# Two transformer layers and a mixture-of-experts block on one core: attention taken chunk by chunk, the second chunk moved beside the first chunk's gathers

## The chip, the cores and the metric

The kernel runs on one core of one Trainium2 chip. The metric is the device time of one execution in microseconds; lower is better. The core has TensorE (PE, matrix products; its weight loads are PEld), VectorE (DVE), ScalarE (ACT), GpSimd (POOL) and SyncE (SP), and 16 DMA engines that all queues share. SP issues the loads and stores of whole blocks, POOL the gathers of rows by index. All numbers are float32.

## The reference

256 tokens of width 1024 (two chunks of 128) go through two layers and then through one block of another kind. Shortened, one layer is:

```python
proj = h @ w_in[l]                        # 1024 -> 1536: qa ka va qb kb vb
qa = rope(rms_norm(qa, qn_g)); ka = rope(rms_norm(ka, kn_g))   # 8 and 2 heads of 64
oa = softmax(qa ka^T / 8) va              # branch 0: all 256 keys
ob = window_sink_attention(qb, kb, vb)    # branch 1: distance bias, |i-j| <= 128, sink
oa = rms_norm(oa, gn_a_g); ob = rms_norm(ob, gn_b_g)           # per head of 64
h = layer_norm(ALPHA * h + concat(oa, ob) @ w_o[l], ln1)
q = h @ peer_wq[l]                        # 1024 -> 2048 = 8 heads x 2 halves x 128
s = q . sub_keys                          # 8 x 2 x 128 scores per token
top 16 of each half, top 16 of the 256 sums -> 128 experts per token
a = gelu(u[expert] . h);  ffn = sum_k softmax(s)_k a_k v[expert_k]
h = layer_norm(ALPHA * h + ffn, ln2)
```

Queries need only their own chunk of tokens; keys and values of both chunks are needed by every query. After the two layers come modulation columns (silu of a condition vector times a 1024 x 6144 matrix), a context of 256 rows that is turned into states of two recurrent mixers, the mixers over the tokens, and 64 experts of which each token uses 8.

## The kernel before

Every engine has a program of its own (`tensor_program`, `vector_program`, `scalar_program`, `gpsimd_program`, `sync_program`). Each runs its instructions in the order in which the Python code emits them. What must wait for another engine names an event (`at("ps", "proj", l, i, c)`), and the wait stands in the order of the waiting engine: all that is queued behind it waits too. L123 is a line of the kernel; most operations are recorded at the line of a helper (L155 matmul, L158 transpose, L76 to L118 DVE, L125 ACT, L134 POOL, L2424 the gather, L1343 the dot product).

For each layer `attention(l)` runs first, for both chunks: h is turned (`hT`), three blocks of `w_in` give the projections of both chunks, `rope` normalizes and rotates queries and keys (DVE one half, POOL the other), `turned_heads` turns each head of 64 by itself, then `scores`, `exps`, `turned_powers` and `values` for two branches and two chunks. The softmax's divisor is applied to the values; `squared` and `normed` make the RMS norm in rows (token by token), the result is turned again (`mT`) and multiplied with `w_o`, and a layer norm follows for each chunk. In layer 0 the twelve blocks of the modulation matrix (`mod_products`, 2 MB each, two places in the ring) are woven between these steps by hand.

Then `peer(l, background)` runs: queries of both chunks (`queries(i, c)`, four blocks of `peer_wq`, each used for both chunks) and key scores in halves, in the order (half 0, chunk 0), (half 0, chunk 1), (half 1, chunk 0), (half 1, chunk 1). DVE's `route(0)` finds the experts of the first 64 gathers as soon as half 0 of chunk 0 is there. Then 256 gathers run, 128 for each chunk: gather n fetches 128 rows of 8 KB (u and v of one expert for each token). DVE takes the dot product of its first half with h (`dots`), ACT makes gelu, weight and a diagonal matrix (`weigh`), PE adds the weighted second half to two accumulators in PSUM (`weighted_sum`). There are eight landing places (`GATHERS`), and POOL issues gather n when PE has used gather n - 8. Between gathers each engine takes pieces of `route(q + 1)` (DVE, every second gather) and of a background generator: `beside(l, n)` says after which gathers one piece is taken. In layer 0 the background is the context's rows and features (40 places, every sixth gather), in layer 1 the context's states (80 places, every third gather, from 10 on). A piece is the same step of one list on every engine.

The ring is 20 places of 4 KB per partition in SBUF for weights and landings, the arena 88 KB per partition for everything else. `sync_program` is one list of loads in a fixed order; each waits for the place that it overwrites, and all loads behind it wait with it.

```python
                for n in range(256):
                    if n % 128 == 0:
                        two = [fresh("acc", l, n // 128, x, among=SUMS[n // 128]) for x in range(2)]
                    weighted_sum(n, two)
                    advance(background, beside(l, n))
```

Of the kernel before, what the change touches and what calls it, by code (L numbers as in the profile page):

```python
# [5 lines left out]
P = 128  # L6
# [188 lines left out]
WQ_AT = (4, 8, 16, 0)  # L195
UNITS = [(0, 0), (0, 1), (1, 0), (1, 1)]
ROUTE_PIECES, EXP_AT, WEIGHTS_AT = 24, 50, 54
NORM_AT = (130, 131, 133, 137, 138)


def beside(l, n):

    if l:
        return 1 if n in range(10, 250, 3) else 0
    return 1 if n in range(10, 246, 6) else 0
# [16 lines left out]
class Side:  # L222


    def __init__(self, x, ar, o, t, rows, convs, convs2=(), convs3=()):
# [3 lines left out]
        self.x, self.tag, self.ar, self.t = x, "x" if x else "ctx", ar, t  # L229
# [8 lines left out]

    def T(self, i, n=1):
        return self.ar(self.t + 512 * i, 512 * n)  # L240
# [58 lines left out]
def build(nc, d, out):  # L299
    import numpy as np  # L300
    ctx = ExitStack()
    with ctx:
# [9 lines left out]
        s_x0, s_cst = [sem(f"x{c}_loaded") for c in range(2)], sem("constants_loaded")  # L312
# [5 lines left out]
        s_gab, s_ctx = sem("gab_loaded"), sem("context_loaded")  # L318
        s_featured, s_feat = sem("features_stored"), sem("features_loaded")
# [40 lines left out]
        def R(i, k):  # L360
# [3 lines left out]
                                                  "b_mod", "cvec", "conv", "norm_cols")}  # L364
        asm = {n: sm(k) for n, k in (("ss0", 10), ("rs0", 10), ("ss1", 10), ("rs1", 10), ("s8", 8))}
        for i in range(2):
            asm |= {f"{n}{i}": sm(k) for n, k in (("ms", 16), ("mr", 16))}
# [14 lines left out]
        ctx_side = Side(False, ar, {"Rk": 9600, "Rv": 10624, "GG": 11648, "GkT": 13696}, 16768,  # L382
                        [("Rk", 0, 16), ("Rv", 1, 16)], [(0, "Gk", 16, 4), (1, "Gv", 16, 8)])
        ctx_rows = ar(11648, 2048).rearrange("p (c n) -> p c n", c=2)
        hcT = ar(14720, 2048).rearrange("p (k t) -> p k t", k=8)
        ctx_tiles = [ar(14720 + 512 * i, 512) for i in range(11)] + [ar(512, 512), None]
        ctx_kd = ar(0, 512)
        ctx_features = ar(9600, 5120)
        norm_scratch = ar(2048, 1024)
        SC = ar(0, 4096)  # L390
        gs, aa = ar(9056, 256), ar(9312, 256)
        diagonals = [ar(8800, 64), ar(8928, 64)]
        mod_rows = ar(20480, 2048)
        silu_cols = ar(19840, 256).rearrange("p (k s) -> p k s", k=8)

        def landing(n):

            i = n % GATHERS
            return R(4 + 2 * i, 2) if i < 5 else ar(6144, 2048) if i == 5 else R(2 * i - 12, 2)
# [2505 lines left out]
```

## Time and profile before

| | us |
|---|---|
| median of 3 runs (2923.17 to 2926.06) | 2924.0 |
| profiled execution, its own time | 2928.04 |
| span of the profiled execution, first to last instruction | 2926.2 |

| engine | busy us | share of the span |
|---|---|---|
| PE | 2148.5 | 73% |
| PEld | 1089.7 | 37% |
| DVE | 1582.8 | 54% |
| ACT | 813.4 | 28% |
| POOL | 843.2 | 29% |

The page also cuts the span into 40 slices of 73 us; each digit is the busy share in tenths (9 is 90% or more), for PEclk the granted clock of TensorE in tenths of full speed, and the last line is what the DMA engines moved.

```profile
PE   6988677666766989676767666789878677667573
DVE  4426857678544645888979865455552522121111
PEclk9889687677866989688888997899989788888887
DMA  7744999999999414999999999412112599999994
GB/s 282 263 169 159 421 422 422 420 412 395 422 422 378 194 37 160 381 421 375 413 378 403 422 421 417 159 42 74 58 62 101 210 404 401 388 391 381 382 379 146
```

The shares are averages over stages with different limits, so they say little by themselves. The stages are told apart by the gathers: slices 4 to 12 and 15 to 24.

### The profile page before, as it was taken

How to read it: one execution, taken by the hardware profiler on the slowest of the kernel's cores; microseconds unless marked ns; L12 is line 12 of the kernel's file. 1: busy time of each engine (PE TensorE's matmuls, PEld its weight loads, DVE VectorE, ACT ScalarE, POOL GpSimd, SP SyncE). 2: the span in 40 equal slices, each digit the busy share in tenths (PEclk: the TensorE clock that was granted, in tenths of full speed). 3: DMA queues.
4: the chain of work that ended last, by engine and by line, in shares of the span. 5: the costliest groups of instructions: out<-in, count | busy, mean ns of one | idle time of the engine just before them, and what ended most of it. 6: DMA issues, size and time to landing. Idle time of an engine off the chain costs nothing.

```text
span 2926.2 us, 33545 instructions
## 1 busy us (share of the span) xinstructions
PE 2148.5 (73%) x11740; PEld 1089.7 (37%) x11740; DVE 1582.8 (54%) x3254; ACT 813.4 (28%) x2292; POOL 843.2 (29%) x723
## 2 busy tenths in 40 slices
PE   6988677666766989676767666789878677667573
PEld 3657111121211559232323221568764532222221
DVE  4426857678544645888979865455552522121111
ACT  1402343433433212343343533322210111111110
POOL 1001444445432100454445553012110111222221
PEclk9889687677866989688888997899989788888887
DMA  7744999999999414999999999412112599999994
GB/s 282 263 169 159 421 422 422 420 412 395 422 422 378 194 37 160 381 421 375 413 378 403 422 421 417 159 42 74 58 62 101 210 404 401 388 391 381 382 379 146
DMA packets 130146, 891.48 MB, mean 305 GB/s; under 512 B 23216, under 2 KB 23600, under 8 KB 31792
## 3 DMA queue, kind: packets, MB, share of 16 engines
q0 software_dynamic: 86976, 553.74, 46.9%
q1 hardware_dynamic: 42992, 335.50, 28.6%
q8 instruction: 95, 1.56, 0.2%
q14 instruction: 83, 0.68, 0.1%
HBM read 880.21 MB, written 40.37 MB: 315 GB/s over the span
## 4 chain that ended last, share of the span: by engine, by line
PE 33%; DMA 33%; DVE 25%; ACT 4%; issue 4%; POOL 2%; SPq 1%; DVEq 0%; ACTq 0%; POOLq 0%
PE ps L155 31%; DMA ring<-in_peer_uv,idx_u 18%; DVE ring L1343 8%; DMA ring<-in_w_gu 6%; DVE arena L76 6%; DMA ring<-in_w_down 3%; ACT arena L125 3%; DMA arena<-in_w_gu 2%; PE ps L158 2%; DVE iu L113 2%; DVE arena L109 2%; DVE arena L1343 1%; DMA arena<-in_w_down 1%; DVE arena L97 1%; DMA arena<-in_peer_uv,idx_u 1%
## 5 line engine op out<-in xcount | busy, mean ns | idle before, releaser
L155 PE MATMUL ps<-ring,arena 64*64 64x512 f32 (+4 forms) x5248 | 1057.6, 764 | 475.2 <-ACT arena L125 348.0
L1343 DVE CUSTOM_DVE_ANT_0 ring<-ring,h 128x1024 f32<-128x1024 f32 x448 | 561.3, 1253 | 298.2 <-DMA ring<-in_peer_uv,idx_u 264.5
L2424 POOL DMA_INDIRECT ring<-in_peer_uv,idx_u x448 | 500.6, 1117 | 676.6 <-PE ps L155 517.4
L155 PEld LDWEIGHTS ps<-ring,arena 64*64 64x64 f32 (+3 forms) x5248 | 264.2, 158 | 1118.3 <-ACT arena L125 762.2
L155 PE MATMUL ps<-arena 128*128 128x128 f32 (+7 forms) x2760 | 471.4, 434 | 133.7 <-ACT arena L125 65.8
L125 ACT ACTIVATE arena<-arena 128x1 f32<-128x1 f32 (+3 forms) x1093 | 294.2, 269 | 812.8 <-DVE arena L1343 693.2
L155 PEld LDWEIGHTS ps<-arena 128*128 128x128 f32 (+4 forms) x2760 | 290.2, 191 | 325.4 <-ACT arena L125 150.7
L76 DVE TENSOR_TENSOR arena<-arena,ps 128x512 f32<-128x512 f32 (+1 forms) x158 | 93.6, 593 | 429.3 <-ACT arena L125 356.3
L155 PE MATMUL ps<-ring,hT 128*128 128x512 f32 (+2 forms) x896 | 310.2, 507 | 15.2 <-DVE hT L97 9.7
L125 ACT ACTIVATE arena<-ps 128x512 f32<-128x512 f32 (+5 forms) x192 | 106.4, 554 | 754.9 <-PE ps L155 707.5
L155 PEld LDWEIGHTS ps<-ring,hT 128*128 128x128 f32 x896 | 173.8, 200 | 140.9 <-issue 115.2
L2561 POOL DMA_INDIRECT y_tab<-arena,iu x64 | 100.2, 1565 | 435.0 <-DVE arena L97 307.7
L134 POOL TENSOR_TENSOR small<-small,cst 128x1 f32<-128x1 f32 (+3 forms) x42 | 46.8, 1114 | 572.4 <-DVE small L84 558.4
L125 ACT ACTIVATE arena<-cst,arena 128x64 f32<-128x64 f32 x512 | 178.0, 348 | 79.0 <-PE ps L155 32.4
L155 PE MATMUL ps<-hT,ring 128*128 128x128 f32 (+1 forms) x1280 | 180.5, 304 | 12.0 <-ACT hT L125 12.0
L155 PEld LDWEIGHTS ps<-hT,ring 128*128 128x128 f32 x1280 | 170.1, 199 | 20.3 <-issue 10.5
L158 PE MATMUL ps<-cst,arena 128*128 128x128 f32 (+1 forms) x706 | 118.2, 317 | 61.1 <-DVE arena L76 32.7
L158 PEld LDWEIGHTS ps<-cst,arena 128*128 128x128 f32 (+1 forms) x706 | 95.1, 160 | 124.9 <-issue 44.9
L97 DVE COPY arena<-ps 128x512 f32<-128x512 f32 (+5 forms) x102 | 59.6, 584 | 149.0 <-PE ps L155 80.7
L134 POOL TENSOR_TENSOR arena<-arena,cst 128x512 f32<-128x512 f32 (+2 forms) x52 | 69.3, 1332 | 222.2 <-DVE arena L76 124.9
L1343 DVE CUSTOM_DVE_ANT_0 arena<-arena,h 128x1024 f32<-128x1024 f32 x64 | 82.1, 1283 | 39.9 <-DMA arena<-in_peer_uv,idx_u 34.3
L2424 POOL DMA_INDIRECT arena<-in_peer_uv,idx_u x64 | 71.6, 1119 | 100.8 <-PE ps L155 97.2
(116 smaller groups left out, 1394.6 us busy)
## 6 DMA issues: line engine op xcount, KB each, us to landing
ring<-in_w_gu SPq DMA_DIRECT2D x98, 1024.0 KB, 28.5
ring<-in_w_down SPq DMA_DIRECT2D x52, 1024.0 KB, 30.7
ring<-in_w_in SPq DMA_DIRECT2D x16, 2048.0 KB, 12.5
arena<-in_w_gu SPq DMA_DIRECT2D x30, 1024.0 KB, 29.9
ring<-in_w_mod SPq DMA_DIRECT2D x12, 2048.0 KB, 7.8
ring<-in_peer_wq SPq DMA_DIRECT2D x8, 2048.0 KB, 7.8
ring<-in_w_o SPq DMA_DIRECT2D x6, 2048.0 KB, 10.4
ring<-in_w_gates SPq DMA_DIRECT2D x12, 1024.0 KB, 4.9
```

The source lines that it names most:

```text
L76: self.done(self.e.tensor_tensor(o, a, b, op), *names)
L97: self.done(self.e.tensor_copy(o, a), *names)
L109: self.done(self.e.max(out=o, in_=a), *names)
L113: self.done(self.e.max_index(o, m, a), *names)
L125: self.done(self.e.activation(o, a, f, **k), *names)
L134: self.done(self.e.tensor_tensor(o, a, b, op), *names)
L155: return self.e.matmul(o, lhsT, rhs, start=start, stop=stop, skip_group_check=True)
L158: return self.e.transpose(o, src, ident)
L1343: v.done(v.e.tensor_tensor_reduce(out=row, in0=row, in1=h[:, n // 128, :], scale=1.0, scalar=0.0, op0=ALU.mult, op1=ALU.add, accum_out=aa[ ...
L2424: g.e.indirect_dma_start(out=landing(n), out_offset=None, in_=d["peer_uv"], in_offset=bass.IndirectOffsetOnAxis(ap=idx_u[:, n:n + 1], axis ...
L2561: g.e.indirect_dma_start(out=y_tab, out_offset=index(m.add_to, n), in_=m.yb[s % 2], in_offset=None, bounds_check=2 * T - 1, oob_is_err=Fal ...
```

## The change

- Attention is done for chunk 0 alone before the gathers of chunk 0 (`first_chunk`); attention of chunk 1, its output rows, layer norm, queries and key scores are a generator (`second_chunk`, 47 pieces in gathers 2 to 71) that runs beside the gathers. The context work follows from gather 72 on: layer 0 every third gather, then every second from gather 222 on, layer 1 every second gather.
- At the end of layer 0's background `next_rows(1)` turns chunk 0 of the new h, projects it, ropes it and turns its keys and queries, so that layer 1 begins with chunk 1's projections only. Its `w_in` blocks are loaded beside the gathers of layer 0.
- Queries are taken chunk by chunk, so each of the four `peer_wq` blocks is loaded twice in each layer, into other places for each chunk (`X_AT`, `Y_AT`).
- Heads are kept in pairs (kv 0 in partitions 0 to 63, kv 1 in 64 to 127; weights reordered on the way in): one transpose of 128 x 128 instead of two of 128 x 64, and the score and value products of a pair use different halves of the array. The softmax's divisor is applied to the powers before they are turned (`scaled`), and values come out turned, so the second turning (`mT`) is gone.
- The norm's factors: ACT squares the values, PE multiplies with a 0/1 matrix of two columns (`spread`) which gives mean squares by token, DVE and POOL make the factors, DVE repeats them 64 times, PE turns them by products with the identity (`spread_back`), and DVE multiplies. ACT applies the gain by columns while it copies.
- The first 144 columns of the constants (identity and exponents) are loaded by themselves, ahead of the rest. The places and the order of the loads change; the modulation's blocks come in two halves of 1 MB in ring places 0 to 3.

```diff
 def beside(l, n):
+    if n < 72:
+        return 1 if n >= 2 and n % 3 else 0
     if l:
-        return 1 if n in range(10, 250, 3) else 0
-    return 1 if n in range(10, 246, 6) else 0
+        return 1 if n < 250 and n % 2 == 0 else 0
+    return 1 if n in range(72, LAST_ROWS, 3) or n in range(LAST_ROWS, 252, 2) else 0
...
+            def spread(l, br, c, among=range(8)):
+                b = fresh("ms", l, br, c, among=among)
+                pe.wait_ge(*at("sq", "mix", l, br, c))
+                for j in range(4):
+                    t = pe.mm(b[:, 2 * j:2 * j + 2], spread_at(br, c)[0][:, j * P:(j + 1) * P], C("group"))
+                pe.done(t, ("ps", "ms", l, br, c))
...
+            def first_chunk(l):
...
+                turned_powers(l, 1, 0, free)
                 modulation(1)
+                values(l, 1, 0, free)
+                turned_powers(l, 0, 0, free)
+                spread(l, 1, 0, free)
                 modulation(2)
+                spread_back(l, 1, 0, free)
+                values(l, 0, 0, free)
+                spread(l, 0, 0, free)
+                spread_back(l, 0, 0, free)
+                run(out_rows(l, 0, free))
                 modulation(3)
+                turned_queries(l, 0, 1, free)
+                turned_queries(l, 1, 1, free)
+                modulation_columns(0)
+                turned_rows(2 * l + 1, 0, free)
+                for i in range(2):
+                    run(queries(l, i, 0, free))
+                key_scores(l, 0, 0, free)
                 modulation(4)
+                run(queries(l, 2, 0, free))
                 modulation(5)
+                run(queries(l, 3, 0, free))
                 modulation(6)
+                key_scores(l, 0, 1, free)
                 modulation(7)
                 modulation_columns(1)
+                modulation(8, 9, 10, 11)
+                modulation_columns(2)
+
+            def second_chunk(l):
+                yield
+                for br in (1, 0):
+                    scores(l, br, 1, OTHERS)
+                    yield from idle(3)
+                    turned_powers(l, br, 1, OTHERS)
+                    yield from idle(2)
+                    values(l, br, 1, OTHERS)
+                    yield
+                    spread(l, br, 1, OTHERS)
+                    yield
+                    spread_back(l, br, 1, OTHERS)
+                    yield from idle(2)
+                yield from out_rows(l, 1, OTHERS)
+                yield from idle(5)
+                turned_rows(2 * l + 1, 1, OTHERS)
+                yield
+                for hf in range(2):
+                    for i in (2 * hf, 2 * hf + 1):
+                        yield from queries(l, i, 1, OTHERS)
+                        yield
+                    key_scores(l, 1, hf, OTHERS)
+                    yield
...
             for l in range(LAYERS):
-                attention(l)
+                first_chunk(l)
                 if l:
-                    peer(l, context_states())
+                    peer(l, chain(second_chunk(l), context_states()))
                 else:
-                    peer(l, chain(context_rows(), conv_features(ctx_side, hcT, ctx_side.conv_blocks, 0, OTHERS)))
+                    peer(l, chain(second_chunk(l), context_rows(),
+                                  conv_features(ctx_side, hcT, ctx_side.conv_blocks, 0, OTHERS), next_rows(1)))
...
+                    elif i >= 6 and l == 0:
+                        for half in range(2):
+                            g.wait_ge(*at("used", "w_mod", 11, half))
+                    elif i >= 2:
+                        g.wait_ge(*at("used", "wq", l, 2 if i < 4 else 3, 0))
...
+            def modulate(*blocks):
+                for i in blocks:
+                    for half in range(2):
+                        load(mod_place(i, half)[:, :], d["w_mod"][i, :, 2048 * half:2048 * half + 2048], mod_sems[half],
+                             ("loaded", "w_mod", i, half), after=[("used", "w_mod", i - 1, half)] if i else ())
...
+                    modulate(5, 6, 7, 8, 9, 10, 11)
+                for i in range(4):
+                    block(Y_AT[l][i % 2], 4, d["peer_wq"][l, i], ("loaded", "wq", l, i, 1),
+                          after=[("used", "wq", l, i - 2, 1) if i > 1 else ("used", "w_o", l, i)])
```

DVE, ACT and POOL have generators of the same names with their share of each piece (DVE: `biases`, `maxima`, `scaled`, `turned_powers`, `mean_squares`, `mix_factors`, `mixed`, `add_rows`, the layer norm; ACT: `exps`, `mix_squares`, copies; POOL: the powers that make the factors, and half of `rope`).

## Rows read from the trace of the kernel before

**Rows 1.** Busy time by stage: us, then busy (instructions) per engine, clock, DMA share, GB/s.

```profile
0.00:260.00 260.00, 223.21 (x1254) 156.07 (x1255) 119.67 (x259) 59.55 (x134) 21.14 (x21) 0.91 0.53 201
260.00:944.00 684.00, 466.79 (x2428) 131.42 (x2426) 448.49 (x928) 255.26 (x824) 283.24 (x261) 0.74 0.99 411
944.00:1155.00 211.00, 184.04 (x971) 138.53 (x968) 114.62 (x244) 47.83 (x114) 19.45 (x16) 0.89 0.31 120
1155.00:1835.00 680.00, 466.48 (x2955) 187.22 (x2954) 533.27 (x1032) 267.74 (x853) 330.15 (x281) 0.84 0.97 399
1835.00:2926.00 1091.00, 807.95 (x4140) 476.50 (x4140) 366.70 (x792) 183.05 (x367) 189.26 (x146) 0.86 0.62 240
```

**Rows 2.** Timeline of POOL: start, us, instruction, idle before and its releaser.

```profile
13.99 2.27 POOL L134 TENSOR_TENSOR small<-small,cst 128x1 f32<-128x1 f32 x2 [13.53 <-DMA cst<-in_consts]
...
259.74 1.17 POOL L2424 DMA_INDIRECT ring<-in_peer_uv,idx_u  x1 [55.81 <-DVE idx_u L97]
...
1154.64 1.02 POOL L2424 DMA_INDIRECT ring<-in_peer_uv,idx_u  x1 [55.21 <-DVE idx_u L97]
```

**Rows 3.** Timeline of PE, prelude of layer 0: projections, scores, output rows.

```profile
22.49 41.44 PE L155 MATMUL ps<-ring,hT 128*128 128x512 f32 x96
...
75.08 7.17 PE L155 MATMUL ps<-arena 64*128 64x256 f32 x32
...
183.55 15.43 PE L155 MATMUL ps<-ring,hT 128*128 128x512 f32 x32 [0.78 <-ACT hT L125]
```

**Rows 4.** Timelines of PE, DVE and POOL, prelude of layer 1.

```profile
953.54 1.97 PE L158 MATMUL ps<-cst,h 128*128 128x128 f32 x8 [8.07 <-DVE h L76]
955.30 42.66 PE L155 MATMUL ps<-ring,hT 128*128 128x512 f32 x96
...
1100.13 16.69 PE L155 MATMUL ps<-hT,ring 128*128 128x128 f32 x128 [4.79 <-ACT hT L125]
...
1039.26 1.65 POOL L134 TENSOR_TENSOR small<-small,cst 128x8 f32<-128x8 f32 x1 [39.88 <-DVE small L84]
...
1078.64 0.69 DVE L89 SCALAR_TENSOR_TENSOR h<-h,ps 128x512 f32<-128x512 f32 x1 [6.18 <-PE ps L155]
...
1084.98 1.23 DVE L76 TENSOR_TENSOR h<-h,ring 128x1024 f32<-128x1024 f32 x1
...
1120.30 0.30 DVE L109 MAX8 arena<-arena 128x8 f32<-128x128 f32 x1 [18.30 <-ACT arena L125]
```

**Rows 5.** Busy time in shorter stretches, columns as in rows 1.

```profile
276.00:860.00 584.00, 395.61 (x2048) 109.38 (x2048) 404.77 (x857) 223.42 (x719) 253.68 (x230) 0.75 1.01 417
1175.00:1200.00 25.00, 17.27 (x71) 4.06 (x72) 19.97 (x56) 7.06 (x26) 10.61 (x10) 0.53 1.01 420
1205.00:1255.00 50.00, 31.66 (x168) 11.51 (x169) 45.55 (x107) 20.26 (x62) 23.47 (x21) 0.73 0.90 363
1505.00:1555.00 50.00, 31.68 (x156) 11.01 (x156) 44.82 (x107) 18.38 (x57) 22.90 (x19) 0.66 0.87 353
1605.00:1655.00 50.00, 35.73 (x262) 13.68 (x255) 43.10 (x73) 23.08 (x74) 27.73 (x22) 0.97 1.01 416
```

**Rows 6.** Timeline of PE, last weighted sums of layer 1.

```profile
1820.28 1.98 PE L155 MATMUL ps<-ring,arena 64*64 64x512 f32 x8 [0.67 <-ACT arena L125]
...
1832.67 1.09 PE L155 MATMUL ps<-ring,arena 64*64 64x512 f32 x8 [0.66 <-ACT arena L125]
```

**Rows 7.** Timeline of POOL and DVE beside each other, gathers of layer 1.

```profile
1374.78 3.46 POOL L134 TENSOR_TENSOR arena<-arena,cst 128x512 f32<-128x512 f32 x2 [6.45 <-DVE arena L76]
1374.84 2.28 DVE L1343 CUSTOM_DVE_ANT_0 arena<-arena,h 128x1024 f32<-128x1024 f32 x1
```

**Rows 8.** Groups by line and form, 1155 to 1835 us, dot products.

```profile
L1343 DVE CUSTOM_DVE_ANT_0 ring<-ring,h 128x1024 f32<-128x1024 f32 x224 | 286.8, 1280 | 109.6 <-DMA ring<-in_peer_uv,idx_u 88.3
```

**Rows 9.** Page, DMA issues: count, KB each, median us to landing.

```profile
ring<-in_w_mod SPq DMA_DIRECT2D x12, 2048.0 KB, 7.8
ring<-in_peer_wq SPq DMA_DIRECT2D x8, 2048.0 KB, 7.8
```

More of the change, by code:

```diff
@@ L494, in modulation @@
+            def first_chunk(l):
+                free = range(6) if l == 0 else range(8)
                 def modulation(*blocks):
@@ L552, in attention @@
+                turned_keys(l, 1, 1)
+                if l == 0:
+                    run(project(0, 2, 0))
+                    turned_queries(0, 1, 0)
+                scores(l, 1, 0)
+                run(project(l, 1, 1))
+                if l == 0:
+                    turned_keys(0, 0, 0)
+                turned_keys(l, 0, 1, free)
+                if l == 0:
+                    turned_queries(0, 0, 0, free)
+                scores(l, 0, 0, free)
                 modulation(0)
-                scores(1, 0, upper)
@@ new lines, in next_rows @@
+            def next_rows(l):
+                take_kt(hT, ("hT", 2 * l), 0, 4)
+                a.wait_ge(*at("features stored"))
+                yield
+                yield from idle(3)
+                take_rows(l, 1, 0)
+                yield
+                yield
+                take_rows(l, 2, 0)
+                yield
+                take_keys(l, 1, 0)
+                take_queries(l, 1, 0)
+                yield from idle(3)
+                take_keys(l, 0, 0)
+                take_queries(l, 0, 0)
+                yield
@@ new lines, in sync_program @@
+                for i in range(2):
+                    block(Y_AT[l][i], 4, d["w_o"][l, i], ("loaded", "w_o", l, i), after=last)
+                into_p(d["peer_keys"][l], ("loaded", "keys", l), [("used", "w_in", l, 0)])
+                norm_rows(2 + 4 * l, "ln1", l, [("used", "ln2", 0) if l else ("used", "ln0", 0)])
+                if l == 0:
+                    modulate(1)
+                for i in range(2):
+                    block(X_AT[l][i], 4, d["peer_wq"][l, i], ("loaded", "wq", l, i, 0), after=[("used", "w_in", l, 1 + i)])
@@ new lines, in sync_program @@
+                if l:
+                    load(ctx_features, d["ctx_tab"], s_feat, ("loaded", "ctx", "features"), after=[("used", "keys", 1), ("features stored",)])
+                else:
+                    load(ctx_rows, rows_of(d["ctx"]), s_ctx, ("loaded", "ctx"), after=[("used", "wq", 0, 3, 1)])
+                    for i, (name, before) in enumerate((("Rk", ("used", "keys", 0)), ("Rv", ("used", "ctx", "Rk")),
+                                                        ("Gk", ("used", "ctx", "Rv")), ("Gv", ("used", "ctx", "Gk")))):
+                        into_p(d["w_in2"][i], ("loaded", "ctx", name), [before])
+                    into_p(d["w_in"][1, 0], ("loaded", "w_in", 1, 0), [("used", "ctx", "Gv")])
@@ L2784, in constants @@
     t["ident"] = np.eye(P)
+    t["mhalf"] = np.full((P, 16), -0.5)
     t["triF"] = (i[:, None] <= i[None, :])
```

1080 lines of the change are left out of this document (583 added, 497 removed).

## The prediction

> **What bounds the kernel now.** I read the busy time by stage first [rows 1]. The program has five stages, and two of them, of 684 and 680 us, are the gathers of the two layers. There the DMA engines are busy for 0.99 and 0.97 of the time at 411 and 399 GB/s, so bytes set their length, while VectorE (DVE) has 448 and 533 us of work. In the two stretches ahead of them (260 and 211 us, here "preludes") the DMA share is only 0.53 and 0.31: attention, the projections and the first routing run alone. The last stage, 1091 us, is touched by nothing but a few places of weights. The timeline of POOL gives the edges: the first gather is issued at 259.74 us because its indices come then, and in layer 1 at 1154.64 after 55.21 us of waiting for DVE [rows 2]. So there are two terms to earn, the preludes, and two to pay, the gather stages.
>
> **Prelude of layer 0 (259.7 us now).** (a) Constants. POOL's first products waited 13.53 us for the constants [rows 2]. With the 144 columns that they need ahead of the rest I put TensorE's (PE's) start at 15 us instead of 19. (b) PE still makes the six projections before the first chunk can finish: 41.4 us [rows 3]. With the turned rows of h (3.7), two waits for copies (4), the transposes of keys and queries (2) and the scores of one chunk (both branches took 7.2 us for 32 instructions [rows 3]; the two heads of a pair now lie in different halves of the array, which I count as nothing gained) that ends at 73. Four blocks of modulation, the turned powers and values of both branches, with their copies, take it to 85. (c) The norm's factors are now a chain for each branch: Square on ACT (0.6), product with the group columns (0.5), DVE (0.2), POOL's power of 8 columns (1.65 [rows 4]), a copy (0.7), the product back (0.5), the product of both (0.7), with the handovers some 6 us each, and the second branch's copies wait behind the first's factors on DVE. Bounds for the two chains: 2 us if they hide each other, 18 us if all is serial; I take 13, near the serial end, since PE's queue holds the output rows behind them. Now 98. (d) Output rows of one chunk: 15.4 us [rows 3], so 113.5. (e) From the last output product to the normed h 7.6 us (1078.64 to 1086.21 [rows 4]), turning and copying 2.5, two blocks of queries 16.7, to the start of routing 3.5, routing 34.3 (1120.30 to 1154.64 [rows 2, 4]): first gather at **178 us**, 82 earlier. Chunk 1's scores, powers, values, mean squares and half of the queries are what has left this path.
>
> But eight blocks of modulation, two more blocks of queries and two sets of columns stand in PE's queue ahead of the first weighted sum, and each block now comes in two halves through only two places of 1 MB, each filled only when the last block has left it. A 2 MB block took 7.8 us to land [rows 9]; I estimate 6 us a block when PE has nothing else. Blocks 7 to 11 then end near 198 us and PE's first weighted sum is at **203 us**. Gathers 6 and 7 wait for those same places. Six gathers (15 us at 422 GB/s) and the last blocks keep the DMA engines half busy meanwhile.
>
> **Gather stage of layer 0.** Bytes before: 256 gathers of 1.05 MB are 268.4 MB, and 12.1 MB for the context (411 GB/s x 684 us = 281 MB [rows 1]). New in it: the four query blocks read a second time for chunk 1 (four of 2 MB [rows 9], 8.4 MB), three blocks of the next layer's w_in (6.3) and two norm rows (1.0): 15.8 MB, or 37 us at the 422 GB/s of the saturated stretch (417 over 276 to 860 [rows 5]). From 203 us there are 250 gathers and 28 MB left: 290 MB, 688 us. To this I add 4 us of ramp, 5 of tail, 3 for waiting on the stored features, and 15 us for the start, as follows. Chunk 2 of attention is 47 background pieces in gathers 2 to 71, and 23 of them (to the output rows) fall by gather 36. DVE's work there: 34 dot products of 1.36 us (1280 ns mean [rows 8] and a read of 0.08), 18 pieces of routing (25 us), biases, maxima, scalings, copies (25 us; each instruction has its like in the preludes) and four places where it waits in the same piece for a product of PE (3 us each): 108 us against 87 us of DMA. Eight landing places give back some 6. End of the stage: **918 us** (944 now).
>
> **Prelude of layer 1 (210.6 us now).** Chunk 0's h is turned, projected and roped beside the gathers of layer 0. Left: h of chunk 1 (PE starts 9.1 us after the last sum [rows 4]), turning 3, three projections instead of six (half of 42.66 us [rows 4], 21.3) with keys, scores and copies between them (10) makes 43.5; powers and values 8.5; the two factor chains 13; output rows 16.5 (cold); then 10.1, 16.7, 3.5 and 34.3 as above: **146 us**, 64 less. What is late next is the same serial chain of norm, queries and routing, 65 us of it, which the change doesn't touch. First gather at 1064.
>
> **Gather stage of layer 1 (680 us now).** Bytes 268.4 + 8.4 + 1.0 + 2.6 (features, until now loaded in the prelude) + 2.1 = 282.5 MB, 670 us. DVE decides the rest. Three 50-us windows with routing and context states show DVE at 45 us and the DMA share down to 0.90, 0.88 and 0.87; two of them are shown [rows 5]. Some 18 us are lost in this way now. The context states' pieces come every second gather instead of every third from gather 72 on, so about 16 us stay lost there, and the 15 us of the start are added as in layer 0; ramp and tail are 11, since all landing places are free at once. 670 + 16 + 15 + 11 = **712 us**. End 1776. Bounds of the start's loss: 0, if the landing places hide it, and 45, if every one of the 47 pieces costs 1 us.
>
> **What the notes say.** Beside a POOL product of two halves (3.46 us for two) the dot product takes 2.28 us where 1.23 is usual [rows 7], and its mean over this stage is 1280 ns for 224 of them [rows 8], some 12 us of stretching in all. [...]
>
> **Sum.** 1776 + 1092 (last sum to the end, unchanged) = 2868 us span against 2926.2. The profiled execution took 2928.0, 1.8 more than its span and 4.0 more than the median of the runs; so 2868 + 1.8 - 4 = **2866 us**. Norm factors, masks in another order, gathered sinks and fewer biases are inside these terms.
>
> **Rivals.** (B) *The landing places hide the second chunk.* The two losses of 15 us vanish, and so do the 16 us of the context states, if their pieces find DVE free: 2820 us. For it: from 276 to 860 the DMA share is 1.01 with DVE at 69% [rows 5]. Against: the windows at 0.87.
> (C) *A convoy of in-order queues.* Each of the 47 pieces stalls one engine by its handovers, 25 us more in each gather stage: 2916 us. For it: ACT must switch between Exp and Gelu, and POOL issues gathers behind powers that wait for DVE.
> (D) *TensorE becomes the bound, slower than before.* Between sparse products its granted clock falls to 0.53 (1175 to 1200 us [rows 5]), half speed, and a weighted sum takes 1.98 us instead of 1.09 [rows 6]. At that level the first 72 gathers ask 143 us of sums and twice 65 us for the second chunk (at full clock scores 7, output rows 14, four blocks of queries 29, the rest 15): 273 us where DMA needs 200, 73 us more in each layer, less the 15 that I counted: 2982 us. It decides from 29 us a layer on. Against: with more to do the clock was 0.97 (1605 to 1655 [rows 5]), and then the same work takes 143 us.
> (E) *It doesn't bring the first gathers forward usefully:* the modulation's half blocks land so late beside the first gathers that sums begin at 230: 2893 us.
>
> **How the numbers follow.** Chances: forecast 0.56 (its own range 2842 to 2890), B 0.14, C 0.18, D 0.07, E 0.05. Faster or slower is told from 0.2% (6 us) on. B, E, the forecast and nearly all of C are faster: 0.90; same 0.03; slower 0.07. The range runs from B's time to just under C's upper part: 2822 to 2912.
>
> **What would show it.** First gather issued near 178 and, in layer 1, 146 us after the last sum of layer 0; first weighted sum of layer 0 near 203; last ones near 918 and 1776. In the windows of gathers 2 to 36 a DMA share of 0.8 to 0.9 with DVE at 90%, then 1.0 until the routing of layer 1. Wrong would be: a share of 1.0 in those windows (B), or one of 0.7 with PE busy near 100% at half clock (D); a last stage other than 1092 us; a total outside 2822 to 2912.

## The result, and the profile after

The changed kernel takes **3031.6 us** (median of 4 runs, 3026.9 to 3033.3) beside 2923.6 us for the kernel before on the same chip (2921.4 to 2926.1): ratio 1.0367, 95% interval 1.0349 to 1.0385. It is slower by 3.7%, where 2866 us and a gain of 2% were forecast. Its profiled execution took 3026.93 us with a span of 3025.1.

The busy time by stage of the changed kernel, with the columns of [rows 1], answers to those rows line by line:

```profile
0.00:184.00 184.00, 143.41 (x748) 88.95 (x748) 89.66 (x219) 42.24 (x93) 18.11 (x25) 0.93 0.62 240
184.00:998.00 814.00, 555.29 (x2932) 198.51 (x2932) 492.55 (x1014) 287.36 (x895) 301.79 (x272) 0.76 0.91 373
998.00:1144.00 146.00, 98.42 (x510) 68.09 (x506) 74.05 (x185) 30.90 (x72) 10.91 (x12) 0.82 0.27 101
1144.00:1926.00 782.00, 527.69 (x3276) 230.70 (x3280) 561.63 (x1084) 292.38 (x911) 338.05 (x284) 0.81 0.89 362
1926.00:3025.00 1099.00, 812.74 (x4148) 480.26 (x4146) 367.99 (x793) 183.04 (x367) 189.41 (x146) 0.86 0.61 238
```

The two preludes gave what was forecast: 260 us became 184, 211 became 146. That is 141 us earned. The gather stages took 232 us back: 684 became 814, 680 became 782. From the end of the last weighted sum (1833.8 and 1927.8 us) to the end of the span it takes 1092 and 1097 us. And no engine is full in those stages: VectorE (DVE) has 61% and 72%, TensorE (PE) 68%, and the DMA engines, which were busy for 0.99 and 0.97 of the time, now have 0.91 and 0.89.

**Bytes and idle time.** Where the DMA share is 1.01 both kernels move 421 GB/s, so GB/s times length over 421 is the time that a stretch's bytes need, and the rest is time in which the DMA engines lacked work. The edges below are the dot products of gathers 0, 72 and 255, first those of the kernel before:

```profile
265.00:463.00 198.00, 132.45 (x695) 36.15 (x694) 132.27 (x299) 74.16 (x238) 81.43 (x77) 0.77 1.00 415
463.00:940.00 477.00, 325.89 (x1675) 89.65 (x1672) 314.99 (x628) 179.65 (x582) 198.07 (x180) 0.73 1.00 414
1160.00:1358.00 198.00, 136.79 (x855) 56.99 (x853) 158.55 (x339) 78.89 (x244) 95.03 (x81) 0.82 0.98 405
1358.00:1830.00 472.00, 321.81 (x2040) 124.72 (x2040) 372.36 (x690) 187.24 (x606) 231.63 (x196) 0.85 0.98 402
```

and those of the changed kernel:

```profile
190.00:473.00 283.00, 189.43 (x1077) 83.28 (x1070) 158.22 (x346) 93.49 (x283) 92.97 (x78) 0.75 0.81 326
473.00:994.00 521.00, 356.37 (x1815) 110.42 (x1814) 332.93 (x666) 193.02 (x609) 204.49 (x191) 0.77 0.98 402
1150.00:1401.00 251.00, 168.78 (x989) 75.27 (x990) 157.22 (x341) 89.56 (x277) 93.29 (x77) 0.78 0.84 342
1401.00:1924.00 523.00, 357.39 (x2282) 155.25 (x2284) 403.41 (x743) 201.97 (x631) 240.06 (x203) 0.84 0.92 375
```

| stretch | time | of it for bytes | idle, before -> after |
|---|---|---|---|
| layer 0, gathers 0 to 71 | 198 -> 283 | 195 -> 219 | 3 -> 64 |
| layer 0, 72 to 255 | 477 -> 521 | 469 -> 497 | 8 -> 24 |
| layer 1, 0 to 71 | 198 -> 251 | 190 -> 204 | 8 -> 47 |
| layer 1, 72 to 255 | 472 -> 523 | 451 -> 466 | 21 -> 57 |

In these stretches (1345 us before, 1578 after) bytes ask 81 us more and idle time 152 us more. Read the DVE column too: in layer 1's first 72 gathers DVE works 157 us of 251, less than before and for a longer time. An engine whose amount of work set the pace would not look like that. The Trainium skill (Perfetto Trace Analysis, "Roofline") calls a kernel latency-bound, by stalls and dependencies, where the utilization of matmuls and of memory are both low. Here stalls cost 64 and 47 us in the first 72 gathers of the two layers while the DMA share is still 0.81 and 0.84, so a share that looks high doesn't rule them out.

**One piece, followed.** The timeline of the changed kernel while the second branch's means are made (start, us, instruction, idle before it and its releaser), rows of every engine:

```profile
321.02 1.68 POOL L2644 DMA_INDIRECT ring<-in_peer_uv,idx_u  x1 [1.65 <-PE ps L155]
...
326.70 4.83 PE L155 MATMUL ps<-arena 64*64 64x512 f32 x16 [2.68 <-ACT arena L125]
...
331.59 0.60 ACT L125 ACTIVATE arena<-ps 128x512 f32<-128x512 f32 x1 [4.94 <-PE ps L155]
332.22 1.57 ACT L125 ACTIVATE arena<-ps,small 128x128 f32<-128x128 f32 x4
...
334.44 0.35 ACT L125 ACTIVATE arena<-cst,arena 128x64 f32<-128x64 f32 x1
334.84 1.99 PE L155 MATMUL ps<-ring,arena 64*64 64x512 f32 x8 [3.30 <-ACT arena L125]
336.75 1.87 PE L155 MATMUL ps<-cst,arena 128*128 128x2 f32 x8
338.66 0.17 DVE L84 TENSOR_SCALAR small<-ps 128x8 f32<-128x8 f32 x1 [9.26 <-PE ps L155]
338.91 1.67 POOL L134 TENSOR_TENSOR small<-small,cst 128x8 f32<-128x8 f32 x1 [16.21 <-DVE small L84]
...
340.77 1.68 POOL L2644 DMA_INDIRECT arena<-in_peer_uv,idx_u  x1 [0.19 <-issue]
```

The products of the values start at 326.70. ACT needs their result before it makes the next diagonals, so it waits 4.94 us; PE's next weighted sum needs those diagonals, so it waits 3.30; DVE needs the product with the group columns that stands behind that sum, so it waits 9.26 with landed rows in hand; POOL reached its power at 322.7, waits 16.21 for DVE, and issues no gather until 340.77. Each wait stands in front of the gathers' own work on its engine, and each engine waits for another one's gather work: no engine is busy throughout, and for 19.75 us, from 321.02 to 340.77, no gather is issued. Over 284 to 334 us the share is 0.71 with DVE busy for 35 of the 50 us, over 334 to 384 it is 0.80.

**The start of layer 0.** The first gather was issued at 184.46 us (178 forecast), the first weighted sum at 230.06 (203 forecast): PE waits for half blocks of the modulation, and gather 6 for its place. Timelines of PE and POOL:

```profile
199.29 1.94 PE L155 MATMUL ps<-ring,arena 128*32 128x512 f32 x8 [8.23 <-DMA ring<-in_w_mod]
...
223.14 6.99 PE L155 MATMUL ps<-cst,arena 128*128 128x2 f32 x32 [0.72 <-ACT arena L125]
230.06 3.69 PE L155 MATMUL ps<-arena 64*64 64x512 f32 x16
...
184.46 1.17 POOL L2644 DMA_INDIRECT arena<-in_peer_uv,idx_u  x1 [59.73 <-DVE idx_u L97]
...
223.23 0.94 POOL L2644 DMA_INDIRECT ring<-in_peer_uv,idx_u  x1 [30.92 <-PE ps L155]
```

### The profile page after: what moved, and what is told of

Read it like the earlier page. It is cut to its first block, busy times and chain, and to the rows that moved or that the text cites. A ratio compares the mean times of both kernels' runs of the same rounds, so it can differ in the third digit from the quotient of the medians.

```text
span 3025.1 us, 33379 instructions
## 1 busy us (share of the span) xinstructions
PE 2137.6 (71%) x11604; PEld 1066.5 (35%) x11604; DVE 1585.9 (52%) x3294; ACT 835.9 (28%) x2338; POOL 858.3 (28%) x739
## 4 chain that ended last, share of the span: by engine, by line
PE 37%; DMA 27%; DVE 24%; ACT 6%; issue 3%; POOL 1%; SPq 1%; DVEq 0%; ACTq 0%; POOLq 0%
PE ps L155 35%; DMA ring<-in_peer_uv,idx_u 11%; DMA ring<-in_w_gu 7%; DVE ring L1483 6%; DVE arena L76 4%; ACT arena L125 4%; DMA ring<-in_w_down 3%; DVE arena L1483 2%; DMA ring<-in_w_mod 2%; DMA arena<-in_peer_uv,idx_u 2%; PE ps L158 2%; DVE iu L113 1%; DVE arena L109 1%; DVE arena L97 1%; DMA arena<-in_w_gu 1%
## 5 line engine op out<-in xcount | busy, mean ns | idle before, releaser
L155 PE MATMUL ps<-ring,arena 64*64 64x512 f32 (+3 forms) x4576 | 927.8, 774 | 500.4 <-ACT arena L125 346.3
L155 PE MATMUL ps<-arena 128*128 128x128 f32 (+8 forms) x3208 | 569.9, 507 | 192.2 <-ACT arena L125 127.9
L2644 POOL DMA_INDIRECT ring<-in_peer_uv,idx_u x384 | 436.6, 1137 | 604.8 <-PE ps L155 559.7
L1483 DVE CUSTOM_DVE_ANT_0 ring<-ring,h 128x1024 f32<-128x1024 f32 x384 | 479.7, 1249 | 244.6 <-DMA ring<-in_peer_uv,idx_u 194.6
L125 ACT ACTIVATE arena<-ps 128x512 f32<-128x512 f32 (+3 forms) x192 | 104.8, 546 | 821.1 <-PE ps L155 749.8
L2644 POOL DMA_INDIRECT arena<-in_peer_uv,idx_u x128 | 148.0, 1156 | 312.0 <-PE ps L155 169.9
L1483 DVE CUSTOM_DVE_ANT_0 arena<-arena,h 128x1024 f32<-128x1024 f32 x128 | 160.4, 1253 | 89.1 <-DMA arena<-in_peer_uv,idx_u 77.6
L158 PE MATMUL ps<-cst,arena 128*128 128x128 f32 x602 | 97.2, 304 | 54.7 <-DVE arena L76 30.8
L158 PEld LDWEIGHTS ps<-cst,arena 128*128 128x128 f32 x602 | 75.8, 155 | 122.1 <-issue 46.2
L97 DVE COPY arena<-ps 128x512 f32<-128x512 f32 (+3 forms) x90 | 52.4, 583 | 120.3 <-PE ps L158 59.8
L134 POOL TENSOR_TENSOR arena<-arena,cst 128x512 f32<-128x512 f32 (+2 forms) x48 | 52.9, 1102 | 210.2 <-DVE arena L76 111.1
```

Source lines behind the costliest of these rows:

```text
L97: self.done(self.e.tensor_copy(o, a), *names)
L125: self.done(self.e.activation(o, a, f, **k), *names)
L134: self.done(self.e.tensor_tensor(o, a, b, op), *names)
L155: return self.e.matmul(o, lhsT, rhs, start=start, stop=stop, skip_group_check=True)
L158: return self.e.transpose(o, src, ident)
L1483: v.done(v.e.tensor_tensor_reduce(out=row, in0=row, in1=h[:, n // 128, :], scale=1.0, scalar=0.0, op0=ALU.mult, op1=ALU.add, accum_out=aa[ ...
```

## The experiments

Each was timed in three rounds beside the kernel before (medians of its runs 2925.2 to 2927.2 us); its ratio to it stands in brackets with the 95% interval. Not all ran on the same chip, so it is the ratios that compare them. Times of stages come from one trace each: in e1 and e12, whose layer 0 is unchanged, its two stretches take 286 and 525, 285 and 526 us, where the changed kernel has 283 and 521, so differences of up to 5 us in a stretch say nothing. The theories: **1, a convoy**: engines that meet inside a piece hold up the gathers (1a: POOL alone does it; 1b: the handovers of all engines). **2**: DVE's amount of work, as the forecast had it. **3**: bytes. **4**, for gathers 72 to 255: the context's work, pushed out of the first 72 gathers, is too dense there.

### e1: layer 1's second attention ahead of the gathers

```
# all four programs, layer 1 only
 first_chunk(l, chunk) ...  advance(chunk, 24)
-peer(l, chain(second_chunk(l), context_states()))
+peer(l, chain(idle(24), chunk, context_states()))
```

> In layer 1 alone, the first 24 pieces of the second chunk (its scores, powers, values, norm factors and output rows) run ahead of the routing and of the first gather instead of beside gathers 2 to 36; what follows keeps its gathers. Theory 1 (convoy: engines that wait for one another inside a piece hold up the gathers): the prelude of layer 1 grows from 146 to about 190 us, the gather stage falls from 782 to about 742, nearly all of the 41 us of DMA idle time in gathers 2 to 36 gone: about 3035 us in all. Theory 2 (only DVE's amount of work, priced at 15 us): the stage falls to 767: about 3060 us. Theory 3 (bytes alone): the stage stays 782: about 3076 us. Layer 0 stays as it is in all three.

Measured: 3039.6 us (1.0385, 1.0368 to 1.0403). From the last dot product of layer 0 to the first of layer 1 it takes 219 us instead of 156, 63 more; from the dot product of gather 0 to that of gather 72 it now takes 194 us instead of 251:

```profile
1218.00:1412.00 194.00, 137.15 (x837) 51.04 (x838) 130.42 (x292) 68.25 (x225) 84.57 (x75) 0.78 1.01 420
1224.00:1310.00 86.00, 57.11 (x284) 10.52 (x288) 69.93 (x175) 30.14 (x107) 38.31 (x35) 0.68 1.01 422
```

A share of 1.01: no idle time at all, with the second chunk's queries and key scores still beside those gathers. So the attention and output rows alone cause it, and they cost 57 us there (47 of idle time, 10 of bytes) to hide 63 us of prelude. Theory 1 is near in total (3035 expected), but by two misses that nearly cancel: 44 us more of prelude were expected and 40 less of gathers. 2 and 3 are off (3060 and 3076). As DVE's 27 us of attention work left the stretch too, e1 doesn't tell the work from its handovers; e4 does.

### e2: no power on POOL for the second chunk

```
-                    mix_rsqrt(l, br, 1)        # GpSimd
-                v.wait_ge(*at("mix rstd", l, br, c))
+                v.wait_ge(*at("mix var" if c else "mix rstd", l, br, c))
```

> GpSimd's two powers for the second chunk are left out (DVE takes the means as they are, so the output rows are not normed by them); nothing else changes. Theory 1a (GpSimd alone: it reaches the power some three gathers early, waits 10 to 16 us for DVE, and issues no gather meanwhile): about 20 us a layer come back, 2992 us. Theory 1b (the handovers of all engines: PE waits for ACT, DVE for PE in the same pieces, GpSimd is only one of them): 3 to 8 us a layer, about 3020 us. Theory 2 (DVE's work) and theory 3 (bytes): 3032 us.

Measured: 3028.0 us (1.0348, 1.0330 to 1.0365), 4 us less than the changed kernel, with intervals that overlap. POOL's two waits for the means are gone (the one that is left is the layer norm's), but where it waited for them it now waits for PE (waits from 230 to 475 us; first the changed kernel's):

```profile
POOL ring L2644 <- PE ps L155: 89.8, 36, 11.7
...
POOL small L134 <- DVE small L84: 31.8, 3, 16.2
...
DVE small L84 <- PE ps L155: 15.2, 2, 9.3
```

```profile
POOL ring L2643 <- PE ps L155: 118.4, 40, 12.2
...
DVE small L84 <- PE ps L155: 15.4, 2, 9.5
...
POOL small L134 <- DVE small L84: 5.8, 1, 5.8
```

26.0 us of waiting for DVE are gone, and 28.6 us are back as waits of the gathers for their places in the ring. Theory 1a falls (2992 us expected). 1b had 3020 us and isn't borne out in size, nor told from 2 and 3 (3032) by this run; what it shows is that POOL was the most visible victim of the meeting, not its cause.

### e3: the query blocks read once

```
-                pe.wait_ge(*at("loaded", "wq", l, i, c))
+                if c == 0:
+                    pe.wait_ge(*at("loaded", "wq", l, i, c))
 ...
-                    block(Y_AT[l][i % 2], 4, d["peer_wq"][l, i], ("loaded", "wq", l, i, 1), ...)
```

(The second chunk's queries are made from what lies in those places.)

> The second reading of the four query blocks is left out in both layers (8.4 MB each; the second chunk's queries are then made from whatever lies in those places). Theory 3 (bytes): 20 us a layer at 415 GB/s, 2992 us. Theories 1 and 2: they are read where the DMA share is 1.0 (gathers 36 to 72), so nearly all of it comes back as well, 2992 to 3000; if the bytes only fill idle time, 3025 to 3032. What it tells is which part of the 100 us is bytes.

Measured: 3014.9 us (1.0313, 1.0292 to 1.0333), 17 us less. None of the expected times is met (2992 to 3000, or 3025 to 3032). Gathers 0 to 71 take 277 us in layer 0 (283) and 238 in layer 1 (251), for 20 us worth of bytes in each; idle time grows to 79 us (64) and 54 (47). Bytes are a real but small part, and not even these come back whole while the handovers last.

### e4: the same work with its handovers apart

```
-        return 1 if n >= 2 and n % 3 else 0
+        return 1 if n >= 2 else 0
 # first branch, piece numbers, before -> now
 # PE scores 0 -> 0, 1        DVE maxima 0 -> 2, 3       ACT exps 1 -> 3, 5
 # DVE scalings 2 -> 5, 7     PE turns 3 -> 6, 8         PE values 5 -> 11
 # ACT squares 5 -> 12        PE spread 6 -> 14          DVE means 6 -> 16
 # POOL power 6 -> 20         DVE factors 7 -> 20        PE back 7 -> 21    DVE product 8 -> 23
```

(The numbers count from the branch's first piece. The old pieces lay at two of three gathers. `spread_at` of the second chunk moves to two dead tiles so that the branches can overlap.)

> All of the change is kept, but the second chunk's steps lie on 70 pieces, one a gather, instead of 47 at two in three, so that what one engine makes is taken by the next one or two pieces later, GpSimd's powers four pieces later, and scores, maxima, exps and scalings go by halves. Same work, same bytes, four more table loads of ACT a layer. Theory 1 (convoy): the idle time in gathers 2 to 36 (46 us in layer 0, 41 in layer 1) falls to about 15 each: about 2975 us. Theory 1a (GpSimd alone): 2990. Theory 2 (DVE's work): within 10 us of 3032, since DVE has the same to do. Theory 3 (bytes): 3032.

Measured: **2965.9 us** (1.0138, 1.0121 to 1.0155), 66 us less than the changed kernel with the same products, bytes and four more table loads of ACT a layer. Busy time of gathers 0 to 71 in both layers:

```profile
190.00:440.00 250.00, 178.22 (x1064) 80.91 (x1060) 157.59 (x346) 98.56 (x285) 86.65 (x75) 0.80 0.92 367
1122.00:1342.00 220.00, 155.45 (x980) 71.42 (x984) 156.82 (x341) 94.95 (x281) 84.91 (x76) 0.85 0.97 391
```

DVE has the same 158 and 157 us of work in 33 and 31 us less time, so its amount was not the bound. The idle time is 32 us (was 64) and 16 (was 47). Only theory 1b had this. Gathers 72 to 255 are as before (525 and 520 us).

A rival is that e4 only thins the attention out, since its pieces reach to gather 43 instead of 36. Gathers 2 to 36 alone, layer 0 and layer 1 of the changed kernel, then of e4:

```profile
224.00:359.00 135.00, 81.07 (x405) 32.74 (x405) 95.11 (x227) 51.44 (x157) 43.29 (x36) 0.69 0.65 249
1156.00:1287.00 131.00, 74.73 (x375) 27.19 (x376) 93.25 (x220) 49.59 (x152) 42.19 (x34) 0.68 0.70 273
...
224.00:332.00 108.00, 74.17 (x415) 29.21 (x419) 93.89 (x224) 57.46 (x165) 43.66 (x36) 0.75 0.87 330
1128.00:1231.00 103.00, 61.64 (x380) 21.46 (x384) 92.42 (x218) 56.44 (x162) 38.47 (x35) 0.80 0.93 369
```

Nearly the same work lies there in both: DVE's differs by 1.2 and 0.8 us, and of PE's products only the first eight of the output rows (5.9 and 5.4 us) and eight of a turning fall after these gathers in e4. Yet they take 27 and 28 us less. So thinning out explains little of it. What e4 doesn't part is the greater distance of the handovers from the cutting of steps into halves, and from PE's products getting shorter as its granted clock rises (0.69 to 0.75, 0.68 to 0.80). A low clock alone doesn't idle the DMA engines: in e1 the same gathers run at 0.68 with a share of 1.01.

### e5 and e6: less background beside the routing; features early

```
+    routing = 66 <= n < 114 or 130 <= n < 178
+    if l: return 1 if n < 250 and (n % 3 == 0 if routing else n % 3) else 0
```

> As e4, and from gather 72 on the background goes by what DVE has beside it: in the gathers with routing (66 to 113, 130 to 177) one piece in three (layer 1) or four (layer 0), elsewhere two in three or one in two; in layer 1 the norm of the first chunk's rows moves from gathers 130 to 138 to 180 to 188. Same work in all. Theory 1b with DVE as the place where it is short (25 us windows with DVE at 91% and a DMA share down to 0.40): gathers 72 to 255 of layer 1 take 490 us instead of 520, those of layer 0 518 instead of 525: about 2930 us. If the context states' own handovers set the time, and not their meeting with the routing: 2960 to 2970.

Measured: 2947.4 us (1.0070, 1.0049 to 1.0091), 19 less than e4. But the place was wrong: gathers 72 to 255 of layer 1 take 518 us instead of 520 (490 expected), and 514 instead of 525 in layer 0 (518 expected). Shifting the context states within their 178 gathers is no cure.

e6 adds to e5: features loaded after the second chunk's squares, DVE's wait for the stored ones two pieces later, the second chunk's masks made in the prelude.

```
-    load(ctx_features, ..., after=[("used", "keys", 1), ("features stored",)])   # after the query blocks
+    load(ctx_features, ..., after=[("sq", 3, 1), ("features stored",)])          # after the second of them
```

> As e5, and: layer 1's features are loaded as soon as the second chunk's norm has squared (near gather 46) instead of after its last key scores; in layer 0 DVE waits for the stored features two pieces later; the second chunk's masks and distances are made in the prelude, where DVE waits for PE. Waits seen so far: 16.6 us of DVE for the features in layer 1, 10.5 in layer 0, and some 3 us of DVE's work a layer in gather 2. If those waits idle the DMA engines: about 10 us in layer 1, 5 in layer 0, 2 more a layer, 18 less than e5 (2912 if that gives 2930). If the landing places cover them: the same as e5.

Measured: 2935.3 us (1.0027, 1.0013 to 1.0041), 12 less than e5 (18 expected); layer 1's gathers 72 to 255 take 506 us (518), layer 0's 516 (514). DVE's wait for the features in layer 1, 16.6 us in the changed kernel and 14.3 in e5, is gone and fits some 10 of the 12. As e6 makes three changes at once, this is read from the place alone.

### e7: the modulation's blocks 5 to 11 not loaded

```
-                for i in blocks:
+                for i in (x for x in blocks if x < 5):
```

> The changed kernel with blocks 5 to 11 of the modulation not loaded (14.7 MB; PE still makes their products, from what lies there), all else as it is. It prices the late start of layer 0's sums (230 us instead of 203). If the modulation's late blocks cost what they delay: first sum near 200, the last dot product of layer 0 near 968 instead of 999, 3005 us. If the convoy of the second chunk takes it back: 3020 to 3030.

Measured: 2997.8 us (1.0243, 1.0219 to 1.0267), 34 less than the changed kernel. The first weighted sum is at 194.7 us, the last dot product of layer 0 at 968 instead of 994. The first 72 gathers take 28 us less:

```profile
188.00:443.00 255.00, 174.29 (x1029) 78.41 (x1022) 157.97 (x345) 91.70 (x280) 91.53 (x77) 0.78 0.84 339
```

Bytes ask 205 us of it (219 before) and 50 are idle (64), so the late blocks cost these gathers 14 us of bytes and 14 of waiting. That 14.7 MB at 421 GB/s are 35 us says little: by this difference some 9 MB of them had landed before the first dot product. The convoy does not take the gain back.

### e8: eight exps of a branch in one piece again (from e6)

```
-                    (3, lambda: exps(l, 1, 1, (0,))), (5, lambda: exps(l, 1, 1, (1,))),
+                    (4, lambda: exps(l, 1, 1)),
```

> As e6, but the eight exps of a branch stand in one piece again (two table loads of ACT less a branch, one block of 10 us instead of two of 6). If the length of the longest block on ACT decides (weighing stands still for it): 5 to 10 us slower than e6. If the sum of ACT's work does: 2 to 5 us faster. If the eight landing places cover either: the same.

Measured: 2934.2 us (1.0026, 1.0013 to 1.0038) against 2935.3: the same. A block of 8.2 us on ACT (247.5 to 255.7 us of layer 0, with its two table loads) is covered where the next engine takes its result two pieces later.

### e9: modulation blocks 4 to 11 in layer 1's prelude (from e8)

```
+def mod_blocks(l, places):        # blocks 0 to 3 in layer 0, 4 to 11 in layer 1
+    return [x + 4 * l for x in places if x < (8 if l else 4)]
```

> As e8, and blocks 4 to 11 of the modulation (16.8 MB), which only the last stage needs, are loaded and multiplied in the prelude of layer 1, where the DMA share is 0.27, in the same places of PE's queue; layer 0 keeps blocks 0 to 3. By e7 (33 us for 14.7 MB) layer 0 gets 36 us shorter; 16.8 MB fit into the 146 us of layer 1's prelude three times over, so it should grow by 0 to 8 us (eight products of 3.4 us in PE's queue, most of them beside the routing): 2934 - 36 + 4, about 2902 us. If the first sums come no earlier because the convoy takes it back: 2925.

Measured: **2910.3 us** (0.9944, 0.9927 to 0.9960): faster than the kernel before by 0.6%, 24 us less than e8 (32 expected). In the traces the last dot product of layer 0 comes 31 us sooner, and from it to the first of layer 1 it takes 162 us instead of 154. Its stages:

```profile
183.00:925.00 742.00, 516.75 (x2818) 181.69 (x2818) 489.22 (x1005) 283.42 (x889) 298.32 (x272) 0.79 0.97 401
925.00:1077.00 152.00, 125.36 (x685) 80.39 (x686) 76.84 (x193) 35.69 (x80) 10.91 (x12) 0.84 0.53 205
1077.00:1812.00 735.00, 510.94 (x3290) 229.38 (x3294) 558.00 (x1078) 292.38 (x911) 336.22 (x284) 0.85 0.94 385
```

### e10: POOL comes later to its pieces (from e9)

```
-                    if n >= 5: advance(background, beside(l, n - 5))
+                    if n >= 7: advance(background, beside(l, n - 7))
```

> As e9, and GpSimd takes its background pieces seven gathers behind its own loop instead of five, and the norm's power three gathers later, so that it comes to them when DVE has made their inputs. In layer 1 it stood 9 to 11 us at a time before DVE with the next gathers behind it. If these waits of GpSimd are what still idles the DMA engines (some 25 us in layer 1, 10 in layer 0): 15 to 25 us less than e9, about 2882. If they are hidden by the eight landing places, or turn into waits of DVE and PE for GpSimd: the same as e9, or up to 10 us more.

Measured: 2913.4 us (0.9957, 0.9940 to 0.9973), the same as e9. Waits of POOL over gathers 72 to 255 of layer 1, first e9, then e10:

```profile
POOL ring L2648 <- PE ps L155: 154.3, 100, 6.7
...
POOL ring L134 <- DVE arena L76: 33.9, 4, 11.1
```

```profile
POOL ring L2648 <- PE ps L155: 195.9, 106, 6.8
...
POOL ring L134 <- DVE arena L76: 3.6, 2, 2.1
```

As in e2: 30 us of waiting for DVE turn into 42 us of waiting for PE's used places, and the stretch takes 504 and 506 us.

### e11: the second chunk's copies from DVE to ACT (from e10)

```
-                for g in range(2, 4):           # ACT; DVE's two go
+                for g in range(0 if c else 2, 4):
```

> As e10, and the second chunk's four copies of turned powers that DVE made (0.7 us each, 2.8 us a layer) are made by ACT. In gathers 2 to 36 DVE is busy 22.5 of 25 us. If DVE's amount of work is what is left there: 3 us a layer, 6 less than e10. If it is not: the same.

Measured: **2907.1 us** (0.9932, 0.9910 to 0.9953), 6 less than e10, as DVE's work would have it. It isn't shown: the intervals of the two overlap, and in the traces 5 of 9 us come from gathers 72 to 255 of layer 1, where the edit changes nothing.

### e12: half the context states left for after the last gather

```
-        return 1 if n < 250 and n % 2 == 0 else 0
+        return 1 if n < 250 and n % 4 == 0 else 0
```

> The changed kernel; only in layer 1 from gather 72 on, the context states' pieces come every fourth gather instead of every second, so that half of them (some 40) are left for after the last gather, where they delay the end. It asks what the 51 us are that gathers 72 to 255 of layer 1 take more than in the kernel before (523 against 472), where those pieces began at gather 10. Theory 4 (the context's work, pushed out of gathers 10 to 71 by the second chunk, is too much beside what is left): gathers 72 to 255 fall to about 480 us, the rest after them costs some 50 to 80 us, the whole is slower, 3040 to 3070 us. If it is something else (the features' late load, the norm of the first rows, the routing's own handovers): gathers 72 to 255 stay above 510 us.

Measured: 3107.8 us (1.0615, 1.0593 to 1.0637). Gathers 72 to 255 of layer 1 take 499 us instead of 523, DMA engines idle for 33 us instead of 57:

```profile
1405.00:1904.00 499.00, 323.95 (x1959) 124.19 (x1958) 364.65 (x684) 189.49 (x609) 229.05 (x196) 0.80 0.96 393
```

499 lies between the two expectations (480, above 510). So theory 4 holds for at most 24 of the 51 us, since only 45 places for such pieces lie there now, where the kernel before had 59; another 15 are bytes (table above), and of the remaining 12 the features' wait can have most (e6). What is left then runs alone: DVE takes up the last sums 110 us after its last dot product, where it was 4 in the changed kernel. That is 106 us instead of the 50 to 80 that I had expected; without gathers beside it the chain of these pieces stands bare.

## Why the prediction was wrong

The span was forecast at 2868 us and came to 3025, 157 more; slower had been given a chance of 0.07. The sums hold but for two slips that move nothing: rival B's time is 2820 by its terms and 2822 in the range, and 281 MB less 268.4 leaves 12.7 for the context, not 12.1. By its own steps:

- **Preludes.** Right within 6.5 us. Step (e) had 178 us and it was 184.5, layer 1's 146 us is met to the microsecond. The parts that left the path and the chain of norm, queries and routing were read rightly from [rows 3] and [rows 4].
- **First weighted sum at 203 us.** Wrong by 27 (rival E's 230). "6 us a block when PE has nothing else" was too little: the waits above show halves landing one after the other behind six gathers. By e7 the late blocks cost the first 72 gathers 28 us, half of it bytes and half waiting.
- **Bytes of the gather stages.** Right within 2%: from 203 us to the end of its stage layer 0 moved 795 us x 373 GB/s = 296.5 MB (290 forecast; half blocks of the modulation, due before 198 us, were still landing until 220), layer 1 782 x 362 = 283.1 (282.5).
- **"15 us for the start" of each gather stage.** This step failed. It added up DVE's work (108 us against 87 of DMA), put 3 us on each of four waits, and subtracted 6 for the landing places. Gathers 2 to 36 took 135 and 131 us with only 95 and 93 of DVE's work in them, 70 and 71% where 90% was forecast. The idle time of the first 72 gathers grew by 61 and 39 us (14 of the 61 are the modulation's, by e7), and e1 (none left without the attention) and e4 (half of it gone with the same work) show what it is: not DVE's sum but products, ACT's squares, DVE's mean and POOL's power in one piece or the next, each queued behind the gathers' work of its engine. A wait of 3 us in such a piece is 9 for DVE and 16 for POOL. The second bound that I gave, 45 us if every piece costs 1 us, holds for layer 1 and is too low for layer 0.
- **"16 us stay lost" beside the context states.** Too small: 57 us of idle time in gathers 72 to 255 against 21 before. e12 gives at most 24 of the 36 to their closer spacing, which I had noticed and not priced; in layer 0, "3 for waiting on the stored features" was 10.5 us in the trace, and 16 us more of idle time in all.
- **Last stage 1092 us.** 1097, as above; the 5 us are not accounted for. From the last dot product on, e1 to e11 take 1096 to 1102 us, the changed kernel 1102 and the kernel before 1096.

Rival C named the mechanism and had 25 us a stage for it. Idle time grew by 77 and 74 us in the stages (with the ramps: 814 us less 721 for bytes is 93, it was 16; 782 less 672 is 110, it was 36), and at least 32 and 31 of these are the convoy's, as e4 takes them away in the first 72 gathers. Rival B falls with shares of 0.81 and 0.84. Rival D does too: over the first 72 gathers PE is busy 189 of 283 us, and e4 does the same products in 250. In gathers 2 to 36 the share is the 0.7 that was named as its sign (0.65 and 0.70), but PE is busy for 60 and 57% there and not near 100%. The granted clock is 0.69 and 0.68, and in the kernel before the same gathers ran at such a clock with shares of 1.01 and 0.95:

```profile
275.00:368.00 93.00, 59.76 (x296) 12.63 (x296) 72.60 (x181) 34.02 (x114) 38.93 (x40) 0.67 1.01 420
1172.00:1268.00 96.00, 66.14 (x354) 22.88 (x350) 84.67 (x200) 35.28 (x114) 44.83 (x39) 0.70 0.95 391
```

Rival E's time of the first sum came true, but it explains at most the 28 us of e7. What I should have drawn from the profile: in windows with a share of 0.90 and 0.87 [rows 5] the DMA engines idled beside background work although DVE was only at 90%; I read them as DVE being full and scaled them with its work.

## What to carry to other kernels

- Work that is moved beside a stream costs its handovers, not its instructions. Where two engines meet in the same piece, each wait is served only after the stream's own work on both queues; take what one engine makes a piece or two later on the next. Here that was worth 66 of 3032 us, for other piece numbers and some steps cut in halves.
- A long wait on the queue that issues the transfers is a poor guide: taking away 26 and 30 us of them (e2, e10) gave 4 us, not clear of noise, and nothing, since the same queue then waited for its places. Ask which engine gives the places back, and what it waits for.
- Before work is pushed into a full stage, look for the work in it that isn't needed there: eight modulation blocks moved into a stage with a DMA share of 0.27 gave 24 us.

## What the runs showed that I had not expected

ACT's block of eight exps with its two table loads of 1.28 us, 8.2 us in which it weighs nothing, costs no more time than two shorter ones (e8), with its result taken two pieces later. Eight landing places, 20 us of gathers, cover one such block; they did not cover engines that stop for each other in turn (e4). And a saturated stretch moves the same whatever lies beside it: 408 to 426 GB/s, mostly 420 to 423, in the 25 us windows of e4, e1 and e8 with a share of 1.01 or 1.02, with routing, queries or context states there or not.
